# Expert stage of a two-block transformer kernel: scored and added rows alternate, three of eight added rows go to TensorE, the first eight gathers start during the query products

## The reference, cut to what matters

```
def peer(h, w_q, sub_keys, u_tab, v_tab):
    q = (h @ w_q).astype(F32).reshape(bsz, length, PEER_HEADS, 2, PEER_HALF)
    s = jnp.einsum("blhsk,hsnk->blhsn", q, sub_keys.astype(F32))
    s1, i1 = lax.top_k(s[..., 0, :], PEER_TOPK)
    s2, i2 = lax.top_k(s[..., 1, :], PEER_TOPK)
    ...
    top_s, pos = lax.top_k(cand_s, PEER_TOPK)
    idx = jnp.take_along_axis(cand_i, pos, axis=-1)
    g = jax.nn.softmax(top_s, axis=-1)
    ...
        u = jnp.take(u_tab, it, axis=0)
        act = jax.nn.gelu(jnp.einsum("td,tkd->tk", xt, u))
        v = jnp.take(v_tab, it, axis=0)
        return jnp.einsum("tk,tkd->td", gt * act, v)
```

## Time and profile before

| | us |
|---|---|
| median of 3 runs | 4043.09 |
| lowest, highest run | 4041.12, 4044.36 |
| profiled execution, its own time | 4041.94 |
| its span in the trace | 4040.2 |
| DVE busy in the span | 2777.7 (69%) |
| PE busy | 2308.6 (57%) |
| POOL busy | 1672.6 (41%) |

### The profile page before, as it was taken

The page is one execution under the profiler, slowest core; times in us unless marked ns, Lnnn a source line. Parts: engine busy times, 40 slices in busy tenths (PEclk is TensorE's granted clock), DMA queues, the critical chain, the costliest instruction groups (busy, mean ns, idle before and its releaser), DMA issues.

```text
span 4040.2 us, 30536 instructions
## 1 busy us (share of the span) xinstructions
PE 2308.6 (57%) x11184; PEld 1797.0 (44%) x11184; DVE 2777.7 (69%) x3729; ACT 837.7 (21%) x1560; POOL 1672.6 (41%) x1970
## 2 busy tenths in 40 slices
PE   7889999987799999979775897820000000000000
PEld 6545558445688976869655796720000000000000
DVE  6764443377655433564784653579999999999998
ACT  1000000123444412444443453410000000000000
POOL 6887772000000000000232000057787767888886
PEclk9889999988899999989887998965555555555555
DMA  7756855525455511544112451469999989999998
GB/s 287 281 215 222 306 213 182 185 104 186 153 189 188 184 67 52 192 150 159 53 47 99 146 209 65 144 269 377 376 422 384 356 325 392 422 422 422 422 422 355
DMA packets 281959, 974.01 MB, mean 241 GB/s; under 512 B 14288, under 2 KB 26448, under 8 KB 212560
## 3 DMA queue, kind: packets, MB, share of 16 engines
q0 software_dynamic: 76592, 551.58, 33.6%
q1 hardware_dynamic: 203808, 413.78, 29.2%
q10 hardware_dynamic: 1408, 6.69, 0.4%
HBM read 957.33 MB, written 14.68 MB: 241 GB/s over the span
## 4 chain that ended last, share of the span: by engine, by line
PE 43%; DVE 24%; POOL 17%; issue 3%; DMA 2%; ACT 2%; DVEq 0%; ACTq 0%; POOLq 0%
POOL ring L2527 15%; DVE arena L2466 7%; PE lin L311 6%; PE lin L445 5%; PE lin L446 5%; PE lin L447 5%; PE lin L477 4%; DVE ring L2452 4%; PE lin L480 4%; PE lin L479 4%; PE lin L334 3%; DVE mod_sums L773 2%; PE lin L1668 1%; DMA ring<-in_peer_u,arena 1%; PE aux L1677 1%
## 5 line engine op out<-in xcount | busy, mean ns | idle before, releaser
L411 DVE TENSOR_TENSOR weight_parts<-ring,weight_parts 128x512 fp32r<-128x512 f32 (+1 forms) x816 | 537.6, 670 | 455.4 <-ACT weight_parts L399 453.9
L2527 POOL DMA_INDIRECT ring<-in_peer_u,arena x256 | 527.0, 2058 | 423.8 <-PE lin L480 300.6
L2527 POOL DMA_INDIRECT ring<-in_peer_v,arena x256 | 568.7, 2222 | 128.3 <-issue 75.6
L2466 DVE SCALAR_TENSOR_TENSOR arena<-ring,arena 128x2048 f32<-128x2048 f32 x256 | 601.5, 2350 | 29.0 <-DMA ring<-in_peer_v,arena 2.8
L2452 DVE CUSTOM_DVE_ANT_0 ring<-ring,arena 128x2048 f32<-128x2048 f32 x256 | 577.7, 2288 | 33.8 <-DMA ring<-in_peer_u,arena 33.3
L399 ACT CAST weight_parts<-ring 128x512 fp32r<-128x512 f32 (+1 forms) x816 | 486.9, 604 | 539.7 <-PE lin L447 303.7
L1965 POOL TENSOR_TENSOR arena<-arena,ring 128x1024 f32<-128x1024 f32 x8 | 27.1, 3386 | 1124.4 <-DVE arena L1946 1124.4
L477 PE MATMUL lin<-parts,weight_parts 128*128 128x256 f32 x1344 | 387.2, 288 | 35.3 <-DVE weight_parts L411 35.3
L311 PE MATMUL lin<-ring,arena 128*128 128x512 f32 (+2 forms) x968 | 384.5, 561 | 5.5 <-DMA ring<-in_w_in_attn 3.1
L479 PE MATMUL lin<-parts,weight_parts 128*128 128x256 f32 x1344 | 384.8, 286 | 0.0
L480 PE MATMUL lin<-parts,weight_parts 128*128 128x256 f32 x1344 | 384.8, 286 | 0.0
(11 more groups left out here) (272 smaller groups left out, 3248.3 us busy)
## 6 DMA issues: line engine op xcount, KB each, us to landing
ring<-in_ada_w SPq DMA_DIRECT2D x48, 2048.0 KB, 8.8
ring<-in_w_in_fourier SPq DMA_DIRECT2D x32, 2048.0 KB, 8.3
ring<-in_w_in_attn SPq DMA_DIRECT2D x18, 2048.0 KB, 11.0
ring<-in_w_kv_mem SPq DMA_DIRECT2D x16, 2048.0 KB, 10.8
ring<-in_w_out_fourier SPq DMA_DIRECT2D x16, 2048.0 KB, 8.0
ring<-in_w_in SPq DMA_DIRECT2D x12, 2048.0 KB, 7.9
ring<-in_w_out_attn SPq DMA_DIRECT2D x8, 2048.0 KB, 8.0
ring<-in_w_out SPq DMA_DIRECT2D x8, 2048.0 KB, 8.0
```

The lines of the kernel that those rows point to most:

```text
L411: c.nc.vector.tensor_tensor(c.w_parts[:, q, 1, 0:w], c.slot(load, L.kc, w)[:, k % L.kc, :], c.w_parts[:, q, 0, 0:w].bitcast(F32), ALU.subt ...
L2466: nc.vector.scalar_tensor_tensor(out=X.H[:, t, :], in0=buf, scalar=X.act[:, t, k:k + 1], in1=X.H[:, t, :], op0=ALU.mult, op1=ALU.add).then ...
L2527: c.nc.gpsimd.indirect_dma_start(X.bufs[q], None, X.tables[table], bass.IndirectOffsetOnAxis(ap=X.idx[:, t, k:k + 1], axis=0)).then_inc(go ...
```

## The change

Four things are changed. (1) One list, `ORDER`, sets the sequence of gathers for all engines: 36 scored rows, then added and scored rows in turn, and 36 added rows at the end; the added rows of tile 0 stand between scored rows of tile 0 and of tile 1. (2) Of the added rows, those with k % 8 in (1, 4, 6), 48 in a tile, go to PE: ACT writes the weight of each position onto a diagonal (identity times column), and four matmuls (diagonal times 512 columns of the row) accumulate in four PSUM banks over the whole tile. `v_finish` adds the four banks to `X.H`. DVE keeps the other 80. (3) The gelu and the multiplication by weights are done per group of 32 slots, and a choice has its steps at fixed places, two scored rows apart, one group ahead. (4) The first 8 gathers go into buffers 1, 3 and 5 (halves that the weight loads leave free) as soon as choice (0, 0) has its indices; this choice is run at 5 steps per `aside()` and the scoring of the 8 rows at up to 5, later 2, beside the query products. On PE the key scores for it stand directly behind the first query product.

```diff
--- before.py
+++ after.py
@@ -2269,9 +2269,55 @@
         self.idx = c.at(25 * K1 + 512, NT, E_SLOTS).bitcast(U32)
         self.bufs = [c.ring[:, i // 2, (i % 2) * D:(i % 2 + 1) * D] for i in range(2 * RING)]
         self.tables = (c.I["peer_u_2"][0], c.I["peer_v_2"][0])
+        self.sums, self.added, self.diag_holder = {}, None, {}
+
+    def diag_of(self, t, k):
+
+        return sum(1 for j in range(k) if on_pe(j)) % 4
 
...
+EARLY = 8
+LAG = HH * TOPK + 4
+PE_ROWS = (1, 4, 6)
+
+
+def gather_order():
+
+    scored = [(t, 0, k) for t in range(NT) for k in range(E_SLOTS)]
+    added = [(t, 1, k) for t in range(NT) for k in range(E_SLOTS)]
+    order = scored[:LAG]
+    for n in range(len(added)):
+        order.append(added[n])
+        order += scored[LAG + n:LAG + n + 1]
+    return order
+
+
+ORDER = gather_order()
+
+
+def gather_buf(n):
+
+    return (1, 3, 5)[n % 3] if n < EARLY else (n - EARLY) % (2 * RING)
+
+
+def on_pe(k):
+
+    return k % 8 in PE_ROWS
+
+
+LAST_PE_ROW = max(k for k in range(E_SLOTS) if on_pe(k))
+
+
+def choice_at(t, k):
+
+    n = t * GROUPS + k // (HH * TOPK) + 1
+    i = k % (HH * TOPK) - EARLY
+    if n == NT * GROUPS or i < 0 or i % 2 or i // 2 > 9:
+        return None
+    return n // GROUPS, n % GROUPS, i // 2
 
 
 def halves(x):
@@ -2311,17 +2357,31 @@
 
 
 def pe_experts(c):
-    pe, X = c.pe, c.experts
+    nc, pe, X = c.nc, c.pe, c.experts
...
     for group, L in enumerate(X.q_lins):
         yield from pe_split_cols(c, L, "ffn_x", X.cols, turn if group == 0 else None)
         if group == 0:
-            pe.side, pe.rate = [pe_choose(c, X, 0, 0)], 2
-    yield from pe.aside(0)
-    for t in range(NT):
-        for group in range(GROUPS):
-            if t or group:
-                yield from pe_choose(c, X, t, group)
+            yield from pe_choose(c, X, 0, 0)
+    for n, (t, table, k) in enumerate(ORDER):
+        if table == 0:
+            choice = choice_at(t, k)
+            if choice is not None and choice[2] == 0:
+                yield from pe_choose(c, X, *choice[:2])
+            continue
+        if k == PE_ROWS[0]:
+            X.sums[t] = []
+            for b in range(4):
+                bank = yield from pe_bank(c, c.lin, ("rows", t, b))
+                X.sums[t].append(bank)
+        if on_pe(k):
+            yield from pe.wait_ge(("diag", t, k), ("got", t, 1, k))
+            for b in range(4):
+                mm = nc.tensor.matmul(X.sums[t][b][:, :], c.diag[:, X.diag_of(t, k), :],
+                                      X.bufs[gather_buf(n)][:, b * 512:(b + 1) * 512],
+                                      start=(k == PE_ROWS[0]), stop=(k == LAST_PE_ROW), skip_group_check=True)
+            names = [("full", ("rows", t))] if k == LAST_PE_ROW else []
+            mm.then_inc(c.pe_full.after(("row_used", t, 1, k), *names), 1)
 
 
 def v_top16(c, lists, vals, idx, n):
@@ -2438,40 +2498,65 @@
         out = v_cols_block(c, L, lambda j: X.qT[:, group * HH:group * HH + 2, :]) if group % 2 == 0 else nothing
         yield from v_split(c, L, x_part if group == 0 else None, out)
         if group == 0:
-            v.side, v.rate = [v_choose(c, X, 0, 0)], 2
+            v.side, v.rate = [v_choose(c, X, 0, 0), v_scored_early(c, X)], 5
+        elif group == 1:
+            v.rate = 2
     yield from v.aside(0)
...
+    chosen = {}
+    for n, (t, table, k) in enumerate(ORDER):
+        if table == 0:
+            if n >= EARLY:
+                yield from v_scored(c, X, n, t, k)
+            choice = choice_at(t, k)
+            if choice is not None:
+                if choice[2] == 0:
+                    v.side = [v_choose(c, X, *choice[:2])]
                 yield from v.aside(1)
-            yield from v.wait_ge(("got", t, 0, k))
-            buf = X.bufs[gathered(t, 0, k) % len(X.bufs)]
-            nc.vector.tensor_tensor_reduce(out=buf, in0=buf, in1=X.hn[:, t, :], scale=1.0, scalar=0.0, op0=ALU.mult,
-                                           op1=ALU.add, accum_out=X.act[:, t, k:k + 1]).then_inc(
-                c.v_out.after(("row_used", t, 0, k)), 1)
-            if k % 3 == 0:
-                yield from v.aside(1)
-        yield from v.aside(0)
-        yield from v.wait_ge(("gelu", t))
-        nc.vector.tensor_tensor(X.act[:, t, :], X.act[:, t, :], X.g[:, t, :], ALU.mult).then_inc(step.after(), 1)
-        yield from v.wait_ge(step)
-        if t == 0:
-            v.side = [v_choose(c, X, 1, group) for group in range(GROUPS)]
-        for k in range(E_SLOTS):
-            yield from v.wait_ge(("got", t, 1, k), ("row_used", t, 1, k - 1) if k else None)
-            buf = X.bufs[gathered(t, 1, k) % len(X.bufs)]
-            nc.vector.scalar_tensor_tensor(out=X.H[:, t, :], in0=buf, scalar=X.act[:, t, k:k + 1], in1=X.H[:, t, :],
-                                           op0=ALU.mult, op1=ALU.add).then_inc(c.v_out.after(("row_used", t, 1, k)), 1)
-            if k % 3 == 0:
-                yield from v.aside(1)
-        yield from v.aside(0)
-        yield from v_rms(c, ("out", t), (("out", t), "squares"), range(t, t + 1))
-        yield from v.wait_ge(("final_g", "in"))
-        nc.vector.scalar_tensor_tensor(out=X.H[:, t, :], in0=X.H[:, t, :], scalar=c.st[:, t:t + 1], in1=X.f_row,
-                                       op0=ALU.mult, op1=ALU.mult).then_inc(step.after(("out", t)), 1)
+            continue
+        group = k // (HH * TOPK)
+        if k % (HH * TOPK) == 0:
+            ks = slice(k, k + HH * TOPK)
+            yield from v.wait_ge(("gelu", t, group))
+            nc.vector.tensor_tensor(X.act[:, t, ks], X.act[:, t, ks], X.g[:, t, ks], ALU.mult).then_inc(
+                step.after(("weights", t, group)), 1)
+            yield from v.wait_ge(step)
+        if not on_pe(k):
+            yield from v.wait_ge(("got", t, 1, k), X.added)
+            nc.vector.scalar_tensor_tensor(out=X.H[:, t, :], in0=X.bufs[gather_buf(n)], scalar=X.act[:, t, k:k + 1],
+                                           in1=X.H[:, t, :], op0=ALU.mult, op1=ALU.add).then_inc(
+                c.v_out.after(("row_used", t, 1, k)), 1)
+            X.added = ("row_used", t, 1, k)
+        if k == E_SLOTS - 1:
+            yield from v_finish(c, X, t)
+
+
+def v_scored(c, X, n, t, k):
+    yield from c.v.wait_ge(("got", t, 0, k))
+    buf = X.bufs[gather_buf(n)]
+    names = [("scored", t, k // (HH * TOPK))] if k % (HH * TOPK) == HH * TOPK - 1 else []
+    c.nc.vector.tensor_tensor_reduce(out=buf, in0=buf, in1=X.hn[:, t, :], scale=1.0, scalar=0.0, op0=ALU.mult,
+                                     op1=ALU.add, accum_out=X.act[:, t, k:k + 1]).then_inc(
+        c.v_out.after(("row_used", t, 0, k), *names), 1)
+
+
+def v_scored_early(c, X):
+    for n, (t, _, k) in enumerate(ORDER[:EARLY]):
+        yield from v_scored(c, X, n, t, k)
+        yield True
+
+
+def v_finish(c, X, t):
+
+    nc, v, step = c.nc, c.v, c.v_step
+    yield from v.wait_ge(("full", ("rows", t)), X.added)
+    for b in range(4):
+        s = slice(b * 512, (b + 1) * 512)
+        nc.vector.tensor_tensor(X.H[:, t, s], X.H[:, t, s], X.sums[t][b][:, :], ALU.add).then_inc(
+            c.v_out.after(("free", ("rows", t, b))), 1)
...
 
 
 def a_experts(c):
@@ -2484,20 +2569,30 @@
         yield from a_split(c, L, x_part if group == 0 else None,
                            a_odd_groups(c, L, X.qT[:, group * HH:group * HH + 2, :]) if group % 2 else nothing)
         if group == 0:
-            a.side, a.rate = [a_choose(c, X, 0, 0, steps=9)], 2
+            a.side, a.rate = [a_choose(c, X, 0, 0, steps=9)], 5
     yield from a.aside(0)
...
+    for n, (t, table, k) in enumerate(ORDER):
+        group = k // (HH * TOPK)
+        if table == 0:
+            choice = choice_at(t, k)
+            if choice is not None and choice[2] == 9:
+                yield from a_choose(c, X, *choice[:2])
+            if k % (HH * TOPK) == HH * TOPK - 1:
+                ks = slice(k + 1 - HH * TOPK, k + 1)
+                yield from a.wait_ge(("scored", t, group))
+                nc.scalar.activation(X.act[:, t, ks], X.act[:, t, ks], ACT.Gelu_apprx_tanh).then_inc(
+                    c.a_step.after(("gelu", t, group)), 1)
+            continue
+        if on_pe(k):
+            q = X.diag_of(t, k)
+            yield from a.wait_ge(("weights", t, group), X.diag_holder.get(q))
+            X.diag_holder[q] = ("row_used", t, 1, k)
+            nc.scalar.activation(c.diag[:, q, :], c.ident[:, :], ACT.Copy, scale=X.act[:, t, k:k + 1]).then_inc(
+                c.a_step.after(("diag", t, k)), 1)
+        if k == E_SLOTS - 1:
+            yield from a.wait_ge(*[("free", ("rows", t, b)) for b in range(4)])
+            yield from a_row_squares(c, ("out", t), lambda t: X.H[:, t, :], range(t, t + 1))
+            yield from a_rstd(c, ("out", t), st_tmp(c, 1))
 
 
...
 def g_experts(c):
     g, X = c.g, c.experts
     got = [Signal(c, f"gather{i}", 16) for i in range(len(X.bufs))]
```

(25 more changed lines are left out.)

24 lines of the change are left out of this document (4 added, 20 removed).

## The result

The changed kernel takes 3976.51 us in the median of four runs (3974.54 to 3980.35), the kernel before 4042.11 us (4036.17 to 4044.36): a ratio of 0.9841, 95% interval 0.9824 to 0.9858. It is 1.6% faster; 3969 us were predicted, with a range of 3952 to 4003. The median fell by 65.6 us, where 74.4 were predicted. The profiled execution is the slowest of the four: 3980.35 us, a span of 3979.0, where the sum gave 3965.8.

What follows compares the result with a forecast made beforehand. It took the expert stage as bound by DMA, with 82 us lost to DVE. First late row at 2692.2, 503 gathers of 2.487 us, 5 lost and the end gave a 3965.8 us span, 74.4 less: 3969 us, range 3952 to 4003.

Steps and rivals of the forecast that it cites:

- main case: Expert stage: bound by DMA from 2692 us on, giving 3969 us; chance 0.70.
- DVE's load: Gathers behind the queries: with 96 added rows off DVE, 64 gathers hold 134 us of DVE work against 159 of DMA.
- So behind the first stretch DMA is the bound everywhere: Expert stage after the opening scored rows: gathers run at DMA's pace, 5 us lost in all, ends 0 and 40.
- DVE falls 10 us behind, which is 4 rows; eight buffers hold that: Rows 9 to 36, scored rows with one choice: 79.4 us of DVE against 69.6 of DMA, the lag absorbed by buffers.
- worth 0.5 us: Early gathers beside the query products: later gathers start 19.4 us later, but eight fewer save 19.9 us.
- 1.4 for a pair of scored rows (4.4 less 3 covered): Query products 3 and 4: delay from DVE scoring two early rows mid-product, weight buffers hiding 3 us of 4.4.
- The cover of PE's holds: Added rows on PE: buffers held 4 to 7 us cost nothing, since queued gathers cover holds up to 10 us.
- POOL almost never waiting for a buffer: Expert stage: a sign that would show the forecast right, alongside DMA share 1.0 and about 422 GB/s.
- The rule against it: Gathers from HBM to SBUF: a skill's limit of about 358 GB/s would bring the last row 223 us later.
- It does nothing: Gathers: alternating tables costs the engines 0.15 us per gather, 75 us in all; chance 0.02.
- DMA still starves: Expert stage: POOL waits behind PE rows and choices, losing 20 to 45 us instead of 5, 3984 to 4009; chance 0.14.
- The queries suffer more: Query products: twice the wait for the first early row and more ACT delay, 10 to 25 us on top; chance 0.05.

Runs made afterwards that it cites:

- e1: The changed kernel without early gathers or scored rows beside the query products, the first choice at two steps per aside as before: 3971.0 us, ratio to before 0.9828.
- e9: e1 with the choices cut into finer steps, 14 of them packed into rows 8 to 22 of a group: 3983.0 us, ratio to before 0.9863.
- e2: The changed kernel with one idle step ahead of the early scored rows, so DVE first does more of the third query product: 3969.2 us, ratio to before 0.9823.
- e6: e1 with six gather buffers in place of eight: 4026.2 us, ratio to before 0.9974.
- e7: The changed kernel with each of TensorE's matmuls for its added rows issued twice: 3993.9 us, ratio to before 0.9894.
- e8: e1 with two of eight added rows on TensorE in place of three: 3976.1 us, ratio to before 0.9854.
- e4: e1 with no added rows on TensorE, so scored and added rows take turns but DVE adds them all: 3991.9 us, ratio to before 0.9885.
- e5: e1 with the order of gathers from before, all scored rows of a tile, then its added rows, TensorE's share kept: 3988.3 us, ratio to before 0.9872.

## Why the prediction was right, and by what it was off

The main case held: 3976.5 us against 3969. The sum was 13.2 us short of the profiled span. Two of its terms make that up, 6.0 in front of the first late row and 7.9 behind it, less 1 for PE's wait at the end; they err the same way, so the total isn't right by two errors that cancel.

- **DVE's load: right.** The DMA engines are the bound nearly everywhere: of the 25 windows of 50 us from 2700 to 3950, 19 have 420 GB/s or more. The last scored row starts at 3872.8, 89.4 us ahead of the last added one; 89 was written.
- **"So behind the first stretch DMA is the bound everywhere", with 5 us lost: mis-sized.** From the first late scored row to the last added one it took 3962.1 - 2698.2 = 1263.9 us, where 503 x 2.487 are 1251.0: 12.9 lost instead of 5. e1 loses as much, 12.6 (its scored row 0 starts at 2669.3, its last added row at 3952.8, 511 gathers), so this has nothing to do with the early gathers. By (422 - rate)/422 the windows hold 9.2 of it: 3.9 from 2700 to 2800, where DVE is busy 49.5 us of 50, 1.2 from 3000 to 3050, 3.4 from 3350 to 3500 around tile 0's norm, and 0.7 elsewhere. Two rows of the trace bear on it:

```profile
2742.89 2.74 POOL L2616 DMA_INDIRECT ring<-in_peer_u,arena  x1 [8.45 <-DVE arena L2537]
...
3419.66 0.36 SPq L2341 DMA_DIRECT2D out<-arena  x1
```

 The step at fault is "DVE falls 10 us behind, which is 4 rows; eight buffers hold that". They don't quite: POOL waited 8.45 us for a buffer, and the rate fell to 414 and 397 GB/s. That wait alone isn't the cause, as e9 shortened it and gained nothing. The second row is the store of tile 0's output, 1 MiB, landed at 3428.9. The same DMA engines carry it, at their pace in 2.5 us, and the rates above count its bytes; the sum has no term for it. The other 1.2 aren't settled.
- **The early gathers, "worth 0.5 us": mis-sized, and of the other sign.** "idx" was written as ready at 2638.6, scored row 1 landed at 2646.8 and product 3 started at 2649.1; measured 2638.0, 2644.5 and 2646.9. So the long wait was right (17.3 us, 20 expected), in part by luck: the row landed 5.6 us after its issue (2638.89), not 8.2. What followed was not right: products 3 and 4 took 43.1 us (2646.9 to 2690.0) where 2649.1 to 2683.5 (34.4) had been worked out. The term at fault is "1.4 for a pair of scored rows (4.4 less 3 covered)": with waits of 2.84 only 1.6 were covered. Waits and a few matmuls of the changed kernel, on TensorE:

```profile
2647.33 0.58 PE L477 MATMUL lin<-parts,weight_parts 128*128 128x256 f32 x1 [17.25 <-DVE weight_parts L411]
...
2647.93 0.42 PE L480 MATMUL lin<-parts,weight_parts 128*128 128x256 f32 x1
2648.14 0.42 PE L477 MATMUL lin<-parts,weight_parts 128*128 128x256 f32 x1
...
2657.73 0.28 PE L479 MATMUL lin<-parts,weight_parts 128*128 128x256 f32 x1
2657.85 0.28 PE L480 MATMUL lin<-parts,weight_parts 128*128 128x256 f32 x1
2660.97 0.58 PE L477 MATMUL lin<-parts,weight_parts 128*128 128x256 f32 x1 [2.84 <-DVE weight_parts L411]
...
2673.01 0.58 PE L477 MATMUL lin<-parts,weight_parts 128*128 128x256 f32 x1 [5.54 <-DVE weight_parts L411]
...
2685.86 0.39 PE L477 MATMUL lin<-parts,weight_parts 128*128 128x256 f32 x1 [2.84 <-DVE weight_parts L411]
```

 TensorE waited 2.84, 5.54 and 2.84 us for the three pairs, and the wait is not all. Behind the first three of these four waits its matmuls start 0.21 us apart (2647.93, 2648.14) instead of 0.12 (2657.73, 2657.85): the granted clock is 0.55 from 2647 to 2654 and 0.57 from 2661 to 2668, and 1.00 from 2654 to 2658 in between. 28, 28 and 18 matmuls ran at the lower of its two levels, 74 x 0.094 = 7 us. The sum had counted 1.4, 5.1 (with the copy) and 1.4, 7.9 in all, where the waits are 11.2: 3.3 more. With the 7 that is 10.3, where 8.7 were missing. The difference is a burst of this kind in the kernel before, behind its own wait of 11.4 us, in product 4, for which 13.5 us were written:

```profile
2650.00:2657.00 7.00, 6.54 (x41) 6.54 (x42) 3.55 (x9) 2.39 (x6) 0.00 (x0) 0.71 0.00 0
```

 Some 17 of its matmuls ran at the lower level, 1.6 us. The Trainium skill, "TensorE: Matmul & The Clock Gate", section "HAM oscillation — how this bites in real kernels", tells of the same with a wait for DMA in place of DVE: the engine is throttled in the wait, and the next burst starts slow. The trace agrees for the first three of the four waits, 0.41 us a matmul behind them and 0.28 elsewhere; behind the fourth the clock was 1.00 (2686 to 2690). That the clock's share would vanish with the waits was not tried apart from them; e1 and e2 shorten both.
- **The cover of PE's holds: right.** A PE row took 6.7 us at the lower clock and 3.67 at the higher (5.66 in the mean); 6.2 and 3.8 had been estimated. No window between 3550 and 3950 lies below 420 GB/s, and only with fewer buffers (e6) or twice the work (e7) does more time go. The sign "POOL almost never waiting for a buffer" was badly chosen. Waits from 2690 us on, total, times, longest:

```profile
PE lin L2380 <- DMA ring<-in_peer_v,arena: 558.6, 84, 10.8
...
POOL ring L2616 <- PE lin L2380: 176.8, 63, 5.0
...
DVE ring L2537 <- DMA ring<-in_peer_u,arena: 143.9, 63, 8.3
...
POOL ring L2616 <- DVE arena L2537: 39.8, 9, 9.8
```

 POOL waited 177 us for PE rows and the DMA engines hardly ran dry, as a queue of gathers stood behind each. An idle issuer is no idle queue; the DMA share tells the two apart. Nor did DVE wait before nearly every row (63 and 72 times of 408): it waits behind a PE row and then does a few rows at once.
- **The end: right.** Four additions 2.5 us, measured 2.48; behind the last addition 11.9, 11.8 written; PE's wait 0, 1 written.
- **The rule against it: falls.** 422 GB/s hold for over 1200 us with two tables in turn. The Trainium skill, "DMA: Bandwidth & Descriptors", section "Where 436 GB/s comes from", has about 358 GB/s for this path; no kernel here was held to it. The Trainium skill, "DMA: Bandwidth & Descriptors", section "Measured (HBM→SBUF, 128 partitions, SWDGE, issued from GpSimd)", calls this each core's share when both cores of the HBM domain stream and has 425 GB/s for one core alone. This program ran on one core, so the prediction held against itself a rule for another case.
- **The rivals.** "It does nothing" falls with the 422 GB/s of turns. "DMA still starves" is what the 7.9 us above are, less the 2.5 of the store, far under its 20. "The queries suffer more" came to 6 us of its 10 to 25, and not by the mechanism written there: the wait for the first row was shorter than written, not twice as long, and the waits behind it, with the slow matmuls, made the 6.

## What to carry to other kernels

Two edits that each take a load off the same bound don't add, and where two loads are equal on average both are lost in turn: ask for room, not for equality (by the prediction's prices DVE had 143 us of work per 159 of DMA in e8, which lost 3 us against e1, and 161 in e4, which lost 24). Work put "for free" beside a stretch is free only on engines that this stretch doesn't wait for: the gathers were, the scoring of what they fetched was not, and three rows fetched early and scored late beat eight scored early by 10.6 us. A wait of TensorE can cost twice, once itself and once in the slow matmuls behind it: three of the four of 2.8 us and more in products 3 and 4 did. And a transfer that shares the engines of the bound, such as the store here, belongs in the sum.

## What the runs showed of the hardware

- TensorE's mean granted clock over a window lay between its two levels (1.2 and 2.4 GHz, 0.50 and 1.00 here) where the engine worked in bursts: 0.66 to 0.70 when busy 44 us of 100 (changed kernel), 0.86 at 68 (e5), 0.80 at 63 (e7), 1.00 at 50 of 50. More work made each matmul cheaper: e7's doubled rows take 8.4 us, not twice 5.7.
- One core, with the program on no other, gathers rows of 8 KiB at 421 to 422 GB/s where DMA is the bound, whether from one table or from two in turn.
- The issue of a gather on POOL takes 0.93 us with free queues and up to 5.2 under back-pressure; the shortest time from issue to landing was 5.6 us in the changed kernel, for the first early gather.
- Once the last gathers are issued the DMA rate falls ahead of the last landings: 305 GB/s from 3950 to 3962.13 in the changed kernel, while its rows are still taken 2.5 us apart (3957.24, 3959.80, 3962.13).
